# Two input projections of a decoder block as seven half-size products each, with weight sums on GpSimd and VectorE

## The reference, cut to what matters

```python
h = rms_norm(x, g_mix[l])                        # x: 512 x 1024
z = h @ w_in[l]                                  # u | v | q_lat | kv_lat | k_rope | gate_a | gate_b
u, v, q_lat, kv_lat, k_rope, gate_a, gate_b = jnp.split(z, offs, axis=-1)
y_a = spatial_gating(jax.nn.gelu(u), jax.nn.gelu(v), ...)   # u, v, gate_a, gate_b: 1024 columns each
y_b = mla_attention(q_lat, kv_lat, k_rope, ...)
merged = jax.nn.sigmoid(gate_a) * y_a + jax.nn.sigmoid(gate_b) * y_b
x = x + merged @ w_o[l]
```

## Time and profile before

| what | value |
| --- | --- |
| time, median of 3 runs | 1111.4 us (1109.51 to 1111.62) |
| the profiled execution: time | 1110.49 us |
| the profiled execution: span | 1108.7 us |
| PE busy over the span | 1092.9 us |
| DVE, ACT, POOL busy | 861.2, 787.0, 423.6 us |

### The profile page before, as it was taken

The page is one execution under the profiler, slowest core; times in us unless marked ns, Lnnn a source line. Parts: engine busy times, 40 slices in busy tenths (PEclk is TensorE's granted clock), DMA queues, the critical chain, the costliest instruction groups (busy, mean ns, idle before and its releaser), DMA issues.

```text
span 1108.7 us, 17836 instructions
## 1 busy us (share of the span) xinstructions
PE 1092.9 (99%) x5488; PEld 914.7 (83%) x5488; DVE 861.2 (78%) x1239; ACT 787.0 (71%) x1270; POOL 423.6 (38%) x477
## 2 busy tenths in 40 slices
PE   7999999999999999999999999999999999999998
PEld 7988888878778888888888888888888888888787
DVE  4535532278765468999999999999999999999865
ACT  6644433357654343888888898889888988888772
POOL 1120000015276003355556555555655555555400
PEclk9999999999999999999999999999999999999999
DMA  7422422112402259999999999999999999999632
GB/s 251 153 76 76 142 85 76 29 57 71 158 1 71 101 225 381 356 377 382 394 393 388 391 393 388 391 391 393 395 396 396 396 394 393 392 393 359 192 151 76
DMA packets 72130, 291.60 MB, mean 263 GB/s; under 512 B 15187, under 2 KB 20598, under 8 KB 47126
## 3 DMA queue, kind: packets, MB, share of 16 engines
q1 hardware_dynamic: 52672, 254.13, 57.3%
q0 software_dynamic: 18768, 34.79, 12.5%
q10 hardware_dynamic: 646, 2.12, 0.5%
HBM read 284.61 MB, written 42.07 MB: 295 GB/s over the span
## 4 chain that ended last, share of the span: by engine, by line
PE 93%; DVE 3%; ACT 2%; POOL 1%; issue 1%; DMA 0%; ACTq 0%; POOLq 0%; DVEq 0%
PE bank L2065 11%; PE bank L2067 11%; PE bank L2066 11%; PE bank L1752 7%; PE bank L1789 6%; PE bank L1793 6%; PE bank L1790 6%; PE bank L2093 5%; PE bank L2091 5%; PE bank L2092 5%; PE bank L2030 5%; PE bank L1743 2%; PE bank L1944 1%; PE bank L2163 1%; PE bank L2165 1%; PE bank L2164 1%
## 5 line engine op out<-in xcount | busy, mean ns | idle before, releaser
L1624 DVE TENSOR_TENSOR arena_r<-arena,win_r 128x1024 fp32r<-128x1024 f32 x252 | 292.0, 1221 | 21.9 <-ACT win_r L1082 19.1
L1082 ACT ACTIVATE win_r<-arena 128x1024 fp32r<-128x1024 f32 x252 | 246.5, 1069 | 0.5 <-DMA resid<-in_w_exp_up 0.5
L2065 PE MATMUL bank<-win_r,work_r 128*128 128x512 f32 x512 | 206.5, 403 | 0.6 <-issue 0.6
L2066 PE MATMUL bank<-win_r,x_low_r 128*128 128x512 f32 x512 | 199.5, 390 | 0.0
L2067 PE MATMUL bank<-arena_r,work_r 128*128 128x512 f32 x504 | 197.4, 392 | 0.0
L1604 DVE TENSOR_TENSOR arena_r<-arena,hT_r 128x1024 fp32r<-128x1024 f32 x128 | 150.5, 1217 | 0.5 <-ACT hT_r L1090 0.5
L733 POOL DMA_INDIRECT moe_sum<-ya,sidx x64 | 111.5, 1743 | 102.7 <-ACT ya L1118 86.0
L1789 PE MATMUL bank<-arena_r,hT_r 128*128 128x512 f32 (+2 forms) x320 | 121.9, 381 | 2.2 <-DVE win_r L1222 2.1
L1790 PE MATMUL bank<-arena_r 128*128 128x512 f32 (+2 forms) x320 | 121.1, 378 | 0.0
L1793 PE MATMUL bank<-win_r,hT_r 128*128 128x512 f32 (+2 forms) x320 | 121.0, 378 | 0.0
L2067 PEld LDWEIGHTS bank<-arena_r,work_r 128*128 128x128 f32 x504 | 94.6, 188 | 21.7
(11 more groups left out here) (321 smaller groups left out, 2213.4 us busy)
## 6 DMA issues: line engine op xcount, KB each, us to landing
arena<-in_w_exp_down SPq DMA_DIRECT2D x64, 1024.0 KB
arena<-in_w_exp_gate SPq DMA_DIRECT2D x63, 1024.0 KB
arena<-in_w_exp_up SPq DMA_DIRECT2D x63, 1024.0 KB
win<-in_w_in SPq DMA_DIRECT2D x8, 2048.0 KB, 7.8
win<-in_w_o SPq DMA_DIRECT2D x2, 2048.0 KB, 7.9
arena<-in_w_ple_gate SPq DMA_DIRECT2D x2, 2048.0 KB, 13.7
arena<-moe_sum SPq DMA_DIRECT2D x7, 512.0 KB, 7.0
win<-in_mla_w_qb SPq DMA_DIRECT2D x4, 576.0 KB, 4.0
```

The lines of the kernel that those rows point to most:

```text
L1082: act.activation(gu_hi[n % 2][:, :, cols], raw[:, :, cols], ACT.Copy).then_inc(gu_hi_r, 1)
L1624: dve.tensor_tensor(low_[:, :, cols], raw[:, :, cols], gu_hi[n % 2][:, :, cols].bitcast(F32), ALU.subtract).then_inc(gu_lo_r, 1)
L2065: pe.matmul(b_, x_hi[:, k, :], w_hi, start=(k == 0), stop=False)
L2066: pe.matmul(b_, x_lo[:, k, :], w_hi, start=False, stop=False)
```

## The change

u and v (w2 to w5) no longer go through `z_chunk`. Each is one product A x B with A the 512 x 1024 activations and B the 1024 x 1024 weights. Both are cut into four quarters: A by token halves and halves of the input rows, B by halves of the input rows and of the columns. Instead of eight quarter products, seven are made (Strassen's scheme in Winograd's order), each of 256 tokens x 512 rows x 512 columns, that is two groups of 12 matmuls, 24 in all. They are called "11", "T1", "T2", "21", "22", "T3", "T4", in this order; p = 0 is v, p = 1 is u. What this needs:

- **row sums** S1 to S4 of the activations, once, each 128x1024 of f32, on DVE (`rows_1` to `rows_4`), each split like any operand (ACT high, DVE low);
- **weight sums** T1, T2, T3 on POOL (`add_weights`, two instructions of 128x1024 for each) and T4 on DVE (`last_weights`, two instructions), from the four raw quarters of B in SBUF. The order on POOL is v: T1, T2, T3, then u: T1, T3, T2;
- **splits** of seven quarters for each of v and u, in two instructions of 128x1024 on ACT (`high_part`) and two on DVE (`low_part`);
- **product sums**, seven steps with two instructions of 128x512 each, on DVE, one input from PSUM (`add_products`). Then gelu runs on the sums in SBUF. The first product is copied out by ACT (`first_product_out`).

Besides: the gain g_mix moves from the weights to the activations. `hT_evac` and `h_evac` take one slice of 128x128 at a time, four for each bank (32 instructions on each engine in place of 8 on ACT and 12 on DVE), and the remaining splits take two slices in one 128x1024 instruction. The raw quarters are loaded as halves of 1 MB into `ya`, the x buffer and `win`; x is overwritten and loaded again (2 MB) before w_o. The loads of the first two quarters stand ahead of `sgu_w` in SP's queue. The angles and latent norms come later on DVE. The PE loop over w2 to w9 is written out.

```diff
+        PRODUCTS = ("11", "T1", "T2", "21", "22", "T3", "T4")
+        PRODUCT_ROW = {"T1": "S1", "T2": "S2", "22": "S4", "T3": "S3"}
+        WEIGHTS_ORDER = [(0, n) for n in ("T1", "T2", "T3")] + [(p, n) for p in range(1, NP) for n in ("T1", "T3", "T2")]
...
@@ gpsimd, behind the affine_select of wsp and ahead of the rotary tables
+            def add_weights(p, name):
+                done = 2 * WEIGHTS_ORDER.index((p, name))
...
+                if name == "T1" and p == 0:
+                    pool.wait_ge(*raw_landed(0, "11"))
...
+                elif name == "T3":
+                    pool.wait_ge(*raw_landed(p, "12"))
+                else:
+                    pool.wait_ge(lo_ready, split_count(LOWS, p, "T1"))
+                for part in range(2):
...
+                    pool.tensor_tensor(dst, src, other, ALU.add).then_inc(weights_added, 1)
+            for p, name in WEIGHTS_ORDER:
+                add_weights(p, name)
...
@@ scalar
-                    act.activation(hT_hi[:, 4 * (T % 2):4 * (T % 2) + 4, t * P:(t + 1) * P],
-                                   bank[4 + T % 2][:, :].rearrange("p (k q) -> p k q", k=4), ACT.Copy).then_inc(hT_hi_ready, 1)
+                    for i in range(4):
+                        k = 4 * (T % 2) + i
+                        last = act.activation(hT_hi[:, k, t * P:(t + 1) * P], bank[4 + T % 2][:, i * P:(i + 1) * P],
+                                              ACT.Copy, scale=gmix[:, k:k + 1])
+                    last.then_inc(hT_hi_ready, 1)
...
@@ vector
+            rows_1()
+            low_part(0, "T1")
+            low_part(0, "11")
+            rows_2()
+            low_part(0, "S1")
+            rows_4()
+            low_part(0, "S2")
+            low_part(0, "T2")
+            last_weights(0)
+            low_part(0, "S4")
+            low_part(0, "21")
+            low_part(0, "22")
+            rows_3()
+            low_part(0, "S3")
...
+            for p in range(NP):
+                add_products(p, "X")
+                add_products(p, "Y")
+                low_part(p, "T3")
+                low_part(p, "T4")
+                add_products(p, "11")
...
+                    low_part(p + 1, "T1", products_done(p, "22"))
+                add_products(p, "12")
...
+                add_products(p, "22")
+                add_products(p, "W")
+                if p + 1 < NP:
+                    low_part(p + 1, "11")
...
+                add_products(p, "21")
...
@@ tensor
-            with pe.Fori(1, W_Q // 2) as i:
+                    for k in range(HK):
+                        if i == 0 and k % 2 == 0:
+                            pe.wait_ge(lo_ready, split_count(LOWS, p, name, k // 2))
...
+            for p in range(NP):
+                for name in PRODUCTS:
+                    product(p, name)
+            pe.wait_ge(sum_read, 12 * (NP - 1) + SUM_READ["12"] + 2)
+            for i in range(FIRST // 2, W_Q // 2):
```

More of the change, by code:

```diff
@@ L1217, in split @@
-            def split(w):
-                n = chunk_width(w)
-                for k in range(KD):
-                    dve.wait_ge(hi_ready, KD * w + k + 1)
-                    dve.scalar_tensor_tensor(v2(win_r[w % 2], 0, KD, n)[:, k, :], v2(win[w % 2], 0, KD, n)[:, k, :],
-                                             gmix[:, k:k + 1], whi_r[:, k, 0:n].bitcast(F32), ALU.mult, ALU.subtract).then_inc(lo_ready, 1)
+                    for i in range(4):
+                        k = 4 * half + i
+                        last = dve.scalar_tensor_tensor(LO_OF[k][:, q], bank[4 + T % 2][:, i * P:(i + 1) * P], gmix[:, k:k + 1],
+                                                        hT_hi[:, k, q].bitcast(F32), ALU.mult, ALU.subtract)
@@ new lines, in h_evac, with row_hi, row_lo, lower_lo @@
+                    last.then_inc(tr_free[T % 2], 1)
+            first, second, upper, lower = slice(0, HT), slice(HT, SEQ), slice(0, HK), slice(HK, KD)
+            S1, S2, S3, S4 = (s_raw[n] for n in ("S1", "S2", "S3", "S4"))
+            def row_hi(ks, q):
+                return hT_hi[:, ks, q].bitcast(F32)
+            def row_lo(k_first, q):
+                return [z[:, :, q].bitcast(F32) for k0, _, z in hT_lo if k0 == k_first][0]
+            def lower_lo(z, q, op):
+                link(dve.tensor_tensor(z[:, 0:2, :], z[:, 0:2, :], row_lo(4, q), op))
+                return dve.tensor_tensor(z[:, 2:4, :], z[:, 2:4, :], row_lo(6, q), op)
@@ new lines, in rows_1, with rows_2 @@
+            def rows_1():
+                for i in range(2):
+                    dve.wait_ge(tr_free[i], NT)
+                link(dve.tensor_tensor(S1, row_hi(lower, second), row_hi(upper, second), ALU.subtract))
+                link(lower_lo(S1, second, ALU.add))
+                dve.tensor_tensor(S1, S1, row_lo(0, second), ALU.subtract).then_inc(combined, 1)
+            def rows_2():
+                dve.wait_ge(combined, 1)
+                link(dve.tensor_tensor(S2, S1, row_lo(0, first), ALU.add))
+                dve.tensor_tensor(S2, S2, row_hi(upper, first), ALU.add).then_inc(combined, 1)
@@ new lines, in rows_3, with rows_4 @@
+            def rows_3():
+                link(dve.tensor_tensor(S3, row_hi(upper, first), row_hi(upper, second), ALU.subtract))
+                link(dve.tensor_tensor(S3, S3, row_lo(0, first), ALU.add))
+                dve.tensor_tensor(S3, S3, row_lo(0, second), ALU.subtract).then_inc(combined, 1)
+            def rows_4():
+                dve.wait_ge(combined, 2)
+                link(dve.tensor_tensor(S4, S2, row_hi(lower, first), ALU.subtract))
+                lower_lo(S4, first, ALU.subtract).then_inc(combined, 1)
@@ new lines, in low_part @@
+            def low_part(p, name, room=None):
+                if room is not None:
+                    dve.wait_ge(pj_done, room)
+                if name[0] == "S":
+                    dve.wait_ge(hi_ready, split_count(HIGHS, p, name))
+                    dve.tensor_tensor(s_lo[name], s_raw[name], s_hi[name].bitcast(F32), ALU.subtract).then_inc(lo_ready, 1)
+                    return
+                for part in range(2):
+                    dve.wait_ge(hi_ready, split_count(HIGHS, p, name, part))
+                    reader = {"11": "T1", "21": "T4", "22": "T2" if p else "T3"}.get(name)
+                    if reader is not None:
+                        dve.wait_ge(*added(p, reader, part))
+                    dve.tensor_tensor(B_LO[p][name][part][1], B_RAW[p][name][part][0], B_HI[p][name][part][1].bitcast(F32),
+                                      ALU.subtract).then_inc(lo_ready, 1)
@@ new lines, in split @@
+            def split(w, ks=range(KD)):
+                n, step = chunk_width(w), 1 if w == 0 else 2
+                for k in ks[::step]:
+                    z = slice(k, k + step)
+                    dve.wait_ge(hi_ready, KD * w + k + step + (4 - 2 * NP if w >= FIRST else 0))
+                    dve.tensor_tensor(v2(win_r[w % 2], 0, KD, n)[:, z, :], v2(win[w % 2], 0, KD, n)[:, z, :],
+                                      whi_r[:, z, 0:n].bitcast(F32), ALU.subtract).then_inc(lo_ready, step)
```

486 lines of the change are left out of this document (391 added, 95 removed).

## The result

The changed kernel takes 1119.26 us in the median (1119.11 to 1121.26), the kernel before 1111.14 beside it: a ratio of 1.008, 95% interval 1.0062 to 1.0097. The profiled execution took 1119.35 us.

A forecast was written before the change was run, and what follows sets the result against it. PE was taken as the bound, busy 1092.9 of 1108.7 us; -10.9 + 0.8 + 0.3 + 17.9 = +8.1 us on the profiled 1110.5 gave 1118.6, put at 1119 us for the median, range 1105 to 1125.

The forecast's parts named there:

- two groups less: PE in u and v: 14 matmul groups instead of 16, at 5.44 us each, -10.9 us if PE never waits.
- start of w1: Before w1: four-piece evacuations on ACT delay w0, the new w1 split gains; PE gets w1 0.8 us late, bounds 0 and 3.
- DVE and PE arrive together: At the first product of u: DVE ends near 84, PE at 83.6, no cover left; +0.3 us.
- POOL's turns: v to "11" of u: long POOL additions alternate with DVE operations having both inputs in SBUF; +17.9 us.
- PE's lower clock: Rival: PE falls to 1.2 GHz in two waits near 4 us, losing about 2.3 us each; 1124 us, chance 0.10.
- The turn: Each 128x1024 POOL addition between two DVE instructions with both inputs in SBUF costs 2.15 us; eight make 17.2.
- whole-instruction 2.40: Upper price of a turn: POOL excludes DVE for its whole 2.40 us instruction, making the term 2 us more.
- DVE's own work: From w1's first piece to the first product of u: 50.6 us of DVE work plus 2 to 3 waiting, ending near 84.
- Six or seven waits, 15 to 20 us in all: Sign of being right: PE waits for DVE, 2 to 4 us each, from "11" of v to "11" of u.
- a wait on ACT: Sign of being wrong: PE waiting on ACT would mean ACT's queue order or a load is late, priced at nothing beyond DVE's lateness.
- additions that cost DVE little: Rival: POOL's long additions give way or fall into gaps beside DVE; 1102 us, chance 0.15.
- half a turn: Rival: a turn costs about 1.2 us, or only half the additions meet DVE's; 1106 to 1114 us, chance 0.12.

The follow-up runs named there:

- e1: Changed kernel with POOL's twelve weight additions kept in place but cut to 32 elements of a row instead of 1024; 1101.42 us, ratio 0.9914.
- e7: Changed kernel with fourteen filling matmuls of 512 columns added on PE in the wait before "11" of u; 1117.58 us, ratio 1.0054.
- e8: e1 with ACT taking each transposed bank out in one instruction without the gain, as before the change; 1099.82 us, ratio 0.9893.
- e9: e6 with T1 of u on POOL started once S3 is summed, and ten filling matmuls before "11" of u; 1108.4 us, ratio 0.9981.
- e11: e9 with DVE making T2 of u and its low part before T3, behind "11" of u; 1108.01 us, ratio 0.9969.
- e10: Changed kernel with each POOL addition of 1024 elements cut into four of 256, one behind the other; 1111.99 us, ratio 1.0009.
- e4: Changed kernel with all six weight sums of POOL made by DVE instead; 1111.9 us, ratio 1.0008.
- e6: Changed kernel with T2 and T3 of v and u on DVE, T1 of u on POOL waiting for S3's low part; 1109.44 us, ratio 0.9984.
- e5: Changed kernel with POOL making the weight sums of u in the order T1, T2, T3 instead of T1, T3, T2; 1117.5 us, ratio 1.0052.
- e12: e11 with seven more filling matmuls on PE, in the wait before "T3" of v; 1107.26 us, ratio 0.997.

## Why the prediction was right, step by step

The sum can be checked term by term at the end of w9, with e1 as the kernel that has all of the change but the long additions:

| term | put down | measured | from |
| --- | --- | --- | --- |
| two groups less | -10.9 | -10.9 | PE full from 110 to 225, the last two w9 evacuations 5.45 apart |
| start of w1 | +0.8 | +1.0 | 31.64, against the earlier trace rows (e1: 31.83, +1.2) |
| DVE and PE arrive together | +0.3 | 0 | e1: no wait at "11" of u, and no time to spare |
| POOL's turns | +17.9 | +17.3 | "11" of u at 101.33, in e1 at 84.01 |
| PE's lower clock | 0 | +1.7 | from "11" of u to the end of w9: 127.07 us, in e1 125.34, in e7 125.48 |
| sum | +8.1 | +9.1 | 228.40 - 219.24 = 9.16 |

- **The turn** is the step that decided, and it held. Between 37.47 and 66.39 us the change needs 16.05 us more than e1 for the same DVE work, and uses up its 0.94 us of waiting: 17.0 / 8 = 2.12 us a turn, against 2.15. The whole-instruction 2.40 would have made 19.2 of it. T1 of v cost 0.7 us (the w1 split takes 3.84, not 3.13), T2 of u 1.3.
- **DVE's own work** came out so exactly (84.01 in e1, "near 84" on record) that the missing cover is real: what DVE was late at the low parts of "11" of u went through to the end.
- **Start of w1.** The net was right, its parts were not: 0.27 us a piece and 3 us for the first evacuation were close (2.3 measured, 26.92 against the earlier trace rows), but by e8 this costs 1.6 us. So the new split of w1 gives 0.6 of it back; how much of that is its larger pieces, and how much that it stands behind two evacuations and not three, no run tells apart.
- **The mis-sized term is the clock**, which I left out of the sum and gave 0.10 as a rival, for two waits at 2.3 us each. The rival's mechanism was there, its price came true once, at 1.7 us: the waits of 4.58, 4.40 and 3.62 us were all followed by the lower level, but after the first two PE was ahead of DVE anyway. The seven v products last 97.56 - 45.79 = 51.77 us, 38.1 of matmuls, 9.8 of waits, and 3.9 of slower pace that only shortened the waits behind it. Only behind the last one, where PE is the bound again, are 1.7 us lost. (For the start I cited a granted clock of 1.00 from the earlier trace rows, which begin at 15 us; the trace of before has 1.00 from 11 to 12 us too, with matmuls of 384 columns 0.32 us apart, so there only the pace shows the level.) The Trainium skill (TensorE: Matmul & The Clock Gate, Part 1) has the array fall to 1.2 GHz after idling; rows of the change and e7 agree, and in e9 and e11 two waits of 2.4 us went either way.
- **Right partly by luck.** The 1.1 us by which w9 was later than the sum did not reach the median: 0.56 was won back behind w9, where both kernels do the same work, and the profiled run lies 0.1 above the median where I had put the median 0.9 above it. That step was also added wrongly: 1118.6 + 0.9 is 1119.5, and I wrote 1119. The nearness of 1119 to 1119.26 is therefore no measure of the sum, which missed by 1.1 us at w9.
- **Signs.** POOL additions of 3.3 us, DVE at 3.3, w9 near 227 (228.4), seven products of u without a wait: right. Six or seven waits, 15 to 20 us in all: wrong in form, four waits and 13.4 us, because the slow pace took up 3.9. One sign of being wrong did show, a wait on ACT (4.58 us). It does not mean what I wrote there: ACT had stood still for DVE, and in e1, with the same order in ACT's queue, the wait is not there.

The other rivals: additions that cost DVE little are e1's 1101.4, within 0.6 us of the 1102 on record, but that is not what a long addition does; "half a turn" is what e10 brought about by cutting them, at 1112.0.

## What to carry to other kernels

Work given to GpSimd is not free for VectorE when both read two operands from SBUF: price it as a turn of GpSimd's length on each VectorE operation it meets (here 2.12 us for 128x1024, where VectorE needs 1.14 to do it itself), and put it beside PSUM inputs, beside waits, or in short pieces, since an operation paid for one piece only here (0.42 to 0.53 us for 128x256). When an engine with half its time free gets work that a full engine waits for, add up its chain to the first meeting point: here 50 us of DVE met 52 us of PE, and of 19 us of delay 17 went through. A wait of PE can cost more than its length if PE is the bound behind it (here 1.7 us more for 3.62); harmless matmuls into the bank that is about to be started anew removed that part in e7.

## What the runs showed that I had not expected

- Additions in quarters cost the path 6 us less than long ones (95.36 against 101.33), although POOL needs twice the time (12 to 13 us for eight pieces, against 6.5 for two long ones): the loss follows the number of VectorE's operations that meet a piece, times the piece's length, not the elements that GpSimd adds.
- The same wait of 2.4 us was followed by a full clock in one profiled kernel (e9) and by 0.66 in the next (e11); a wait of 2.63 us in e4 was followed by a full clock, one of 2.69 in e6 by the lower level. Part of the spread between runs (1116.41 to 1118.93 in e5) may come from that: its runs with a mean clock of 0.997 took 1116.4 and 1116.7, those with 0.993 to 0.995 took 1117.5 to 1118.9. In e9 and e11 the mean clock does not sort the times in this way, so this is not shown.
- What bounds e12 is mostly no longer the turns: its w9 ends 6.8 us behind e1's (216.13 against 209.35), of which by estimate four additions on DVE ahead of "11" of u make 4.6 (4 x 1.14) and the new wait 0.9; the start of w1 costs both 1 us or so. Whether the row sums could be made in the time before w1, where DVE is at 3.93 of 10 us, was not tried, nor another place for T3 of u.
